# Layer 2's triangular inverse: x and y products in four quadrants of the array

## The reference, cut to what matters

```
C = 64                                    # chunk
a_mat = where(strict, (k*beta) @ k.T * decay, 0) + eye(C)
sol = triangular_solve(a_mat, [v*beta, k*beta*exp(g)], lower=True)
u, w = sol[..., :DV], sol[..., DV:]
def step(s, xs):                          # over the chunks
    v_new = u_c - w_c @ s
    o = qd_c @ s + qk_c @ v_new
    s = s * ge_c + ke_c.T @ v_new
```

## Time and profile before

| | |
|---|---|
| median of 3 runs | 2121.32 us (2121.18 to 2121.86) |
| profiled execution, its own time | 2117.72 us |
| its span in the trace | 2115.9 us |
| TensorE busy | 2023.8 us, 96% of the span |
| VectorE busy | 1547.1 us, 73% |
| ScalarE busy | 913.4 us, 43% |
| mean granted TensorE clock | 0.983 |

### The profile page before, as it was taken

One profiled execution on the slowest core, in us unless ns is written; L12 is line 12 of the kernel. 1 busy time (PEld: TensorE's weight loads), 2 busy tenths in 40 slices (PEclk: granted clock), 3 DMA queues, 4 the chain that ended last, 5 costly groups with the idle time before them and its releaser, 6 DMA issues. The chain is left out here.

```text
span 2115.9 us, 40356 instructions
## 1 busy us (share of the span) xinstructions
PE 2023.8 (96%) x16832; PEld 1782.8 (84%) x16832; DVE 1547.1 (73%) x2438; ACT 913.4 (43%) x1379; POOL 142.6 (7%) x231
## 2 busy tenths in 40 slices
PE   7999999999999999999999999999999999999997
PEld 5787777888888678789888999889899978989997
DVE  6875648899767668766646777789787777967555
ACT  2445553322222244422225544555654445655443
POOL 0100000010110001201220001000000100000000
PEclk7999999999999999999999999999999999999999
DMA  8542013455554176200003677443358844333552
GB/s 330 209 144 85 2 60 120 161 198 177 193 204 148 65 269 220 80 4 3 3 3 131 245 276 277 166 160 140 140 204 277 274 149 170 126 114 140 179 182 96
DMA packets 59135, 323.95 MB, mean 153 GB/s; under 512 B 6384, under 2 KB 7536, under 8 KB 32624
## 3 DMA queue, kind: packets, MB, share of 16 engines
q1 hardware_dynamic: 33360, 228.97, 30.3%
q0 software_dynamic: 25344, 92.29, 12.3%
q10 hardware_dynamic: 288, 0.66, 0.1%
HBM read 320.84 MB, written 1.05 MB: 152 GB/s over the span
## 5 line engine op out<-in xcount | busy, mean ns | idle before, releaser
L372 DVE TENSOR_TENSOR w_low<-raw,w_high 128x1024 fp32r<-128x1024 f32 (+1 forms) x408 | 475.4, 1202 | 151.1 <-ACT w_high L364 150.7
L364 ACT ACTIVATE w_high<-raw 128x1024 fp32r<-128x1024 f32 (+1 forms) x408 | 402.8, 1034 | 333.8 <-PE banks L409 322.6
L550 DVE SCALAR_TENSOR_TENSOR mod_rows<-mod_rows,silu_condition 128x1024 f32<-128x1024 f32 x162 | 196.0, 1221 | 2.6 <-ACT silu_condition L453 1.0
L407 PE MATMUL banks<-ffn_pre_scaled_l,w_high 128*128 128x258 f32 x640 | 180.6, 282 | 0.4 <-DVE w_low L372 0.4
L409 PE MATMUL banks<-ffn_pre_scaled_h,w_low 128*128 128x258 f32 x640 | 180.6, 282 | 0.0
L408 PE MATMUL banks<-ffn_pre_scaled_h,w_high 128*128 128x258 f32 x640 | 180.3, 282 | 0.0
L409 PE MATMUL banks<-mlp_hidden_h,w_low 128*128 128x512 f32 (+1 forms) x512 | 173.2, 338 | 0.0
L408 PE MATMUL banks<-mlp_hidden_h,w_high 128*128 128x512 f32 (+1 forms) x512 | 173.1, 338 | 0.0
L407 PE MATMUL banks<-mlp_hidden_l,w_high 128*128 128x512 f32 (+1 forms) x512 | 173.1, 338 | 0.0
L536 POOL DMA_DIRECT2D mod_rows<-rows_dram x162 | 86.1, 532 | 1238.5 <-DVE mod_rows L550 1045.0
L407 PE MATMUL banks<-mix_l,w_high 128*128 128x256 f32 (+1 forms) x448 | 129.5, 289 | 3.3 <-DVE w_low L372 2.3
(11 more groups left out here) (634 smaller groups left out, 5168.6 us busy)
## 6 DMA issues: line engine op xcount, KB each, us to landing
raw<-panels_dram SPq DMA_DIRECT2D x204, 1024.0 KB, 4.8
mod_rows<-rows_dram POOLq DMA_DIRECT2D x162, 512.0 KB, 5.3
mod_0a_rows<-rows_dram SPq DMA_DIRECT2D x8, 1024.0 KB, 19.4
odd_k_tok<-rows_dram POOLq DMA_DIRECT2D x14, 512.0 KB, 4.9
x_features<-x_features_dram SPq DMA_DIRECT2D x1, 2048.0 KB, 11.1
constants<-small_dram SPq DMA_DIRECT2D x1, 1672.5 KB, 6.6
silu_condition<-conditions_dram SPq DMA_DIRECT2D x2, 512.0 KB, 12.3
out_dram<-x_features SPq DMA_DIRECT2D x4, 256.0 KB, 2.1
```

The lines of the kernel that those rows point to most:

```text
L364: self.nc.scalar.activation(self.wh[:, m % 2, cols], self.raw[:, slot, cols], ACT.Copy).then_inc(self.w_high, 1)
L372: self.nc.vector.tensor_tensor(self.wl[:, m % 2, cols], self.raw[:, slot, cols], self.wh[:, m % 2, cols].bitcast(F32), ALU.subtract).then_ ...
L407: self.nc.tensor.matmul(out, sh(k), ml(k), start=(opens and k == 0), stop=False)
L550: nc.vector.scalar_tensor_tensor(row if v == nv - 1 else self.scratch[:], row, 1.0, self.cond[v][:], ALU.mult, ALU.mult, accum_out=mod[:, ...
```

## The change

Y and T are now kept in the half of the partitions opposite to that of their system, while X and Dt stay. So a T product reads rows of one half and writes to columns of the other; an x product reads the rows of the opposite half and writes back to its own; a y product stays in the opposite half, rows and columns. The x and y products of a direction go out alternately (x, x, y, y for each head), so that four successive products use the four 64x64 quadrants of the array, and both signals come at the end of the 64. In level 0 Y can no longer be copied from `Dt` in place: `first_products` multiplies each `Dt` with the identity in both ways, which gives its transpose for X and a moved plain copy for Y, and `y_out` becomes one full copy from PSUM. The ring has eight sets more (`"ty"` in level 0). `first_products` of the second direction waits for the corner's copies (`corner_out`), a wait that stood ahead of T(1) of level 1.

```diff
-            for kind in ("t", "xy") if n else ("t",):
+            for kind in ("t", "xy") if n else ("ty",):
...
+        def first_products(u, a):
+
+            if u == 0:
+                pe.wait_ge(kt_ready, 2 * a + 2)
+            pe.wait_ge(d_ready, each(u, a))
+            if a and u:
+                pe.wait_ge(corner_out, 2 * u)
+            turned, plain = eight(ring["t", u, 0, a]), eight(ring["y", u, 0, a])
+            for s in range(H):
+                for h, _ in crossed:
+                    nc.tensor.matmul(turned[h, s, :], Dt[h, a, s, h], c("eye64")[h, :], start=True, stop=True)
+                for h, o in crossed:
+                    last = nc.tensor.matmul(plain[o, s, :], c("eye64")[h, :], Dt[h, a, s, h], start=True, stop=True)
+            last.then_inc(t_done, 1)
+
         def t_products(u, n, a):
             dst = eight(ring["t", u, n, a])
-            if u == 0 and n < 2 and a == 0:
-                pe.wait_ge(kt_ready, 2 * n + 2)
-            if n == 0:
-                pe.wait_ge(d_ready, each(u, a))
-            else:
-                pe.wait_ge(xo, t_at(u, n - 1, a))
-                if a and n == 1 and u:
-                    pe.wait_ge(corner_out, 2 * u)
-                elif a and n >= 2:
-                    pe.wait_ge(yo, t_at(u, n - 1, 0))
+            pe.wait_ge(xo, t_at(u, n - 1, a))
+            if a:
+                pe.wait_ge(yo, t_at(u, n - 1, 0))
             for s in range(H):
-                for h in halves:
-                    last = nc.tensor.matmul(dst[h, s, :], Dt[h, a, s, h], X[h, a, s, :] if n else c("eye64")[h, :],
-                                            start=True, stop=True)
+                for h, o in crossed:
+                    last = nc.tensor.matmul(dst[o, s, :], Dt[h, a, s, h], X[h, a, s, :], start=True, stop=True)
             last.then_inc(t_done, 1)
 
         def xy_products(u, n, a):
             pe.wait_ge(t_out, copied(u, n, a))
-            pe.wait_ge(yo, t_at(u, n - 1, a))
-            for what, done in (("x", x_done), ("y", y_done)):
-                dst = eight(ring[what, u, n, a])
-                if n >= 2:
-                    pe.wait_ge(yo, t_at(u, n - 1, 1))
-                for s in range(H):
-                    for h in halves:
-                        st, mv = (Y[h, u % 2, a, s, :], T[h, a, s, :])
-                        if what == "y":
-                            st, mv = mv, st
-                        last = nc.tensor.matmul(dst[h, s, :], st, mv, start=True, stop=True)
-                last.then_inc(done, 1)
+            pe.wait_ge(yo, t_at(u, n - 1, 1))
+            to_x, to_y = eight(ring["x", u, n, a]), eight(ring["y", u, n, a])
+            for s in range(H):
+                for h, o in crossed:
+                    last_x = nc.tensor.matmul(to_x[h, s, :], Y[o, u % 2, a, s, :], T[o, a, s, :], start=True, stop=True)
+                for h, o in crossed:
+                    last_y = nc.tensor.matmul(to_y[o, s, :], T[o, a, s, :], Y[o, u % 2, a, s, :], start=True, stop=True)
+            last_x.then_inc(x_done, 1)
+            last_y.then_inc(y_done, 1)
...
-                for h in halves:
-                    last = nc.scalar.activation(Yf[h, d, :, h], Y[h, u % 2, d], ACT.Copy)
+                for h, o in crossed:
+                    last = nc.scalar.activation(Yf[h, d, :, h], Y[o, u % 2, d], ACT.Copy)
...
-                nc.vector.copy_predicated(Y[:, u % 2, a], spread(lev[a][:, n, :].bitcast(U32), 1, H),
-                                          eight(ring["y", u, n, a])).then_inc(yo, 1)
-                return
-            dve.wait_ge(y_eye, u + 2)
-            dve.wait_ge(d_ready, each(u, a))
-            for h in halves:
-                last = nc.vector.copy_predicated(Y[h, u % 2, a], spread(lev[a][h, 0, :].bitcast(U32), 1, H),
-                                                 Dt[h, a, :, h])
-            last.then_inc(yo, 1)
+            else:
+                dve.wait_ge(t_done, t_at(u, 0, a))
+                dve.wait_ge(y_eye, u + 2)
+            nc.vector.copy_predicated(Y[:, u % 2, a], spread(lev[a][:, n, :].bitcast(U32), 1, H),
+                                      eight(ring["y", u, n, a])).then_inc(yo, 1)
```

More of the change, by code:

```diff
@@ L2299, in odd_mixer @@
     corner_rows = ((halves[0], halves[1]), (halves[1], halves[0]))
+    crossed = ((halves[0], halves[1]), (halves[1], halves[0]))
     paired = [(r, b) for b in range(4) for r in range(2)]
@@ L2429, in corner_first @@
                 for a, (j, i) in enumerate(corner_rows):
-                    last = nc.tensor.matmul(dst[i, s, :], Dt[j, a, s, i], X[j, a, s, :], start=True, stop=True)
+                    last = nc.tensor.matmul(dst[j, s, :], Dt[j, a, s, i], X[j, a, s, :], start=True, stop=True)
             last.then_inc(corner_t, 1)
@@ L2437, in corner_second @@
                 for a, (j, i) in enumerate(corner_rows):
-                    last = nc.tensor.matmul(dst[j, s, :], T[i, 0, s, :], Y[i, u % 2, a, s, :], start=True, stop=True)
+                    last = nc.tensor.matmul(dst[j, s, :], T[j, 0, s, :], Y[j, u % 2, a, s, :], start=True, stop=True)
             last.then_inc(corner_y, 1)
@@ L2500, in _ @@
                 for a in range(2):
-                    t_products(u, n, a)
+                    if n:
+                        t_products(u, n, a)
+                    else:
+                        first_products(u, a)
                 if n:
```

## The result

| | before | changed kernel |
|---|---|---|
| median | 2121.59 us, 4 runs (2121.18 to 2122.40) | 2098.22 us, 4 runs (2097.07 to 2102.67) |
| profiled execution, its own time | 2117.72 us | 2097.74 us |
| its span | 2115.9 us | 2096.0 us |

The ratio is 0.9906, interval 0.9894 to 0.9918: the change gains 23 us by the medians and 20.0 by the profiled executions. 36 were forecast, and 2098.2 lies 1.2 above the range. The direction was right and four quadrants do run at the forecast rate, but not for long; the size was wrong. So the question is where 16 us went.

What follows compares the result with a forecast made beforehand. TensorE's rate of small products was taken to bound a level; -37.4 + 1.1 + 0.9 + 0.6 + 2.8 - 4.1 = -36.1 us, from 2117.7 to 2081.6, or 2085.2 against the median. Range 2079 to 2097.

Steps and rivals of the forecast that it cites:

- Part 1: Levels: 40 pairs of x and y sets take 0.935 us each in four quadrants instead of 1.87, 37.4 us less.
- rival C: Changing quadrant within the same rows drains the array, a pair takes 3.74 us; about 2203 us, chance 0.05.
- A: Rival: four quadrants gain nothing, 29.2 ns for each matmul stays; about +0.5 us, 2121.8, chance 0.07.
- the floor of 25 ns for each matmul: Trainium skill's minimum from one matmul to the next; a pair would take 1.6 us, the kernel about 2110.
- x and y of the same rows going one behind the other: By the skill's rule, weight loads overlap running matmuls only in another row group; no size given.
- Rival B: Instruction supply limits each matmul to between 16.4 and 29.2 ns; at the middle, 22.8, -17 us or 2104, chance 0.08.
- Part 2: Levels of step 0: T(1) waits 0.38 us longer for VectorE's X copy, bare three times; 1.1 us back.
- Part 3: Behind level 5 of step 3: `corner_first` waits for the later Y(1), 1.93 us instead of 1.08; 0.9 back.
- Part 4: Step 2, level 4: VectorE gets to `scores_out` later and `row_sums` waits for it; 0.6 us back.
- Part 5: Steps 1 and 2: `key_products` waits for ScalarE's row decays of the second direction, 1.38 us twice; 2.8 back.
- Part 6: Level 0: 0.9 us less, four times, 3.6 to 5.7 over all with a possible clock stretch; 4.1 less taken.
- Part 7: `y_in_place`, the corner's sets, GpSimd and DMA queues: same counts and shapes or nothing new, no change.

Runs made afterwards that it cites:

- m1: Separate program without the model: streams of 1024 load and matmul pairs with nothing to wait for; four quadrants at 64 columns took 27.29 us, two quadrants 29.86.
- e3: Changed kernel with both directions' row decays on ScalarE ahead of the exponentials of E in steps 2 and 3; 2096.34 us, ratio 0.9898 to the kernel before.
- a1: The changed kernel itself, unaltered, run and profiled once more; 2097.84 us, ratio 0.9902 to the kernel before.
- e4: Changed kernel with the corner's two copies moved from VectorE to ScalarE in steps 0 to 2; 2096.30 us, ratio 0.9891 to the kernel before.
- e6: Changed kernel plus the edits of e3 and e4, with the plain half of `first_products` as one 512-column product per half; 2089.49 us, ratio 0.9856, again 0.9855.
- e2: Changed kernel with the x products in one set, then the y products in another, halves still crossed; 2110.71 us, ratio 0.9959 to the kernel before.
- e7: e6 plus three unused wide products on TensorE ahead of the second `first_products` of steps 1 to 3; 2098.40 us, ratio 0.9895 to the kernel before.

## Why the prediction was right in kind and wrong in size

**Part 1, the pairs, is the step that failed**, and it is the term that decides. The rate was right: 14.7 ns, no cost for changing quadrant within the same rows, so rival C is out, and A too. With them go the floor of 25 ns for each matmul, which the prediction priced at about 2110, and x and y of the same rows going one behind the other. What failed is "40 x (1.87 - 0.935)", the 37.4: from first to last start the 40 pairs took 44.9 us for 72.7 before, 27.8 less, and the holes behind them took some 6 more back. The step takes a rate read from 28 matmuls for the rate of a stretch of hundreds. 28 matmuls say nothing on how fast instructions arrive; m1 first stopped behind its 159th pair. In the levels the holes take about 12 us back, most of the 13.3 by which these fell short. Rival B named the limit, "by the supply of instructions", and put 2104 at the middle of its bounds, 5.8 above the result, where my forecast lies 13.0 below it; I gave it 0.08, since eight instructions start together in rows 4, which shows what is there already, not what comes next. It also missed the form: not a slower rate for each matmul but full rate and then a stop, so it can't be seen in a short window.

**Part 2** (VectorE's chain, 1.1 us): the copies follow at 0.62, as forecast (905.39, 906.01 above). But the wait of T(1) for X that I added to step 0 has no row among TensorE's waits, while step 0 has holes. That these hide the wait was not tested.

**Part 3** (corner of step 3 waits for Y(1), 0.9): right. VectorE and TensorE there, in the timeline:

```profile
1085.29 0.71 DVE L2727 COPY_PREDICATED odd_Y<-constants,banks 128x512 f32<-128x512 uint32 x1
...
1086.14 1.15 PE L2435 MATMUL banks<-odd_X,odd_D 64*64 64x64 f32 x32 [1.83 <-DVE odd_Y L2727]
```

From the last x or y start to the corner it is 2.05 us, before 1.14 (and 1.08 by the earlier trace rows).

**Part 4** (`row_sums` behind the scores): right in kind, a wait of 0.9 us on odd_QKt; from the scores' last start to `row_sums` 1.13 us, before 0.70, so 0.4 for the forecast 0.6.

**Part 5** (row decays late for `key_products`, 2.8): right. From its start to its last start 3.2 us, before 1.8, in two steps; the chain of waits has 2.3, and e3 removes it. e3's median can't say what that was worth: its ratio of 0.9898 has an interval of 0.0043, 9 us from end to end, and the wait is 2. Its trace keeps the time saved, as shown above.

**Part 6** (level 0, -4.1): 0.7 came. Where the clock stayed full the mechanism held: 10.73 less the forecast 0.9 is 9.9, and the runs have 9.87 (a1) and 9.86 (e3), and with a hole in level 0 10.44 (changed kernel, a hole of 0.5) and 10.48 (e3). What failed is that 0.9 was taken four times whatever the clock, and 0.5 more for a stretch at 1.2 GHz that might not come. Windows in level 0 of steps 1, 2 and 3:

```profile
935.50:939.50 4.00, 4.00 (x123) 4.00 (x114) 2.30 (x4) 0.60 (x1) 0.00 (x0) 0.57 0.01 4
989.00:993.00 4.00, 2.49 (x137) 2.34 (x136) 1.34 (x2) 0.60 (x1) 0.00 (x0) 1.00 0.02 4
1037.70:1041.70 4.00, 3.55 (x101) 3.58 (x103) 2.97 (x5) 0.00 (x0) 0.00 (x0) 0.58 0.02 4
```

Two of three at 1.2 GHz, as before, and each such level 0 takes 11.05 to 11.30 instead of 9.9 to 10.5. Before had them in steps 2 and 3, after in 1 and 3: step 1 lost 0.6, step 2 gained 1.0, and step 3, at the lower clock in both, gained 0.1. Step 0, also at the lower clock in both, gained 0.1 (6.33 for 6.41); in a1 it kept the full clock and took 4.95. A TensorE that works faster between the same waits idles no less there; the traces of e4 to e6, which shorten the wait itself, show no such stretch in level 0.

**Part 7** (nothing elsewhere) stands: no new row of the chain of waits is from it.

## What to carry to other kernels

A rate read from some thirty small matmuls is the rate of what has been fetched. Ask also how many instructions the stretch needs: here 256 arrive in 3.4 to 3.7 us, a load and a matmul are two, and an f32 product is two pairs. Where small products already run near 29 ns for each pair, as here, a better packing pays only in bursts, behind work with few instructions. Fewer and wider instructions can pay outside their own place, in what they leave fetched for the next stretch (e6). A kernel bound so may give back part of a wait that is removed, as e4's trace suggests and e3's does not, so judge it by the sum over the stage and not by the wait alone.

## What the runs showed of the hardware that was not expected

- The supply of TensorE's instructions as a limit: a 16 KB packet for every 256 instructions, each 3.4 to 3.7 us (single ones up to 4.0); four quadrants at 64 columns average 26.7 ns over 1024 pairs, and 29.1 behind the first stop, though they run at 14.7 between the stops (m1). That the packets' pace is a limit and not only a consequence of TensorE's demand follows from the stops; what sets the pace was not found.
- Products of a free quadrant start ahead of earlier issued ones of a busy quadrant (e2), and crossing the halves without alternating gives 0.4%.
- Whether a level 0 falls into a stretch at 1.2 GHz varies between executions of the same kernel: steps 1 and 3 in one, 2 and 3 in the other. Each costs about 1 us there. What would keep it away was not settled; e7 did not test it, since e6 had none.
